# The low part of every other weight chunk: a subtraction on VectorE, or a negated copy on ScalarE with an adding DMA of GpSimd

## What is computed

```python
h = x
h = h + gla_mixer(rmsnorm(h, gla_norm), w_in, ...)     # h @ w_in [2048 x 6160], gated linear attention, @ w_out [2048 x 2048]
h = h + square(relu(rmsnorm(h, mlp_norm) @ w_up)) @ w_down   # [2048 x 8192], [8192 x 2048]
h = rmsnorm(h, final_norm)
proj = rmsnorm(h, norm_gain_2) @ w_in_2                # [2048 x 6144]
q, k, v, g_sb, x_lru, g_lru = split(proj)
y = concat(stick_breaking_attention(q, k, v) * silu(g_sb), rg_lru(conv(x_lru)) * silu(g_lru))
return h + y @ w_out_2                                 # [2048 x 2048]
```

## Time and profile before

| | us |
|---|---|
| two runs | 1515.21, 1518.2 |
| median of the runs | 1516.7 |
| profiled execution, first to last instruction (span) | 1514.3 |
| TensorE busy | 1497.6 |
| VectorE busy | 843.5 |
| ScalarE busy | 711.9 |
| GpSimd busy | 30.8 |

### The profile page before, as it was taken

The page is one execution under the profiler, slowest core; times in us unless marked ns, Lnnn a source line. Parts: engine busy times, 40 slices in busy tenths (PEclk is TensorE's granted clock), DMA queues, the critical chain, the costliest instruction groups (busy, mean ns, idle before and its releaser), DMA issues. The chain is left out here.

```text
span 1514.3 us, 19184 instructions
## 1 busy us (share of the span) xinstructions
PE 1497.6 (99%) x6826; PEld 1237.1 (82%) x6826; DVE 843.5 (56%) x872; ACT 711.9 (47%) x856; POOL 30.8 (2%) x54
## 2 busy tenths in 40 slices
PE   7999999999999999999999999999999999999998
PEld 6788888888888888888888888888888888888886
DVE  5555545555555545555555554555566776565653
ACT  5544544445444433443344433444654664565532
POOL 3000000000000000000000000000000011000000
PEclk9999999999999999999999999999999999999999
DMA  8455565657666666666666666666556566545564
GB/s 267 137 167 154 145 202 176 187 176 240 192 183 182 192 192 194 185 182 188 194 189 184 189 190 191 189 190 185 182 180 181 154 194 191 166 144 167 181 193 140
DMA packets 144721, 277.03 MB, mean 183 GB/s; under 512 B 10800, under 2 KB 10912, under 8 KB 144512
## 3 DMA queue, kind: packets, MB, share of 16 engines
q1 hardware_dynamic: 143056, 271.75, 59.3%
q0 software_dynamic: 1040, 3.07, 0.6%
q10 hardware_dynamic: 544, 1.05, 0.2%
HBM read 273.74 MB, written 2.10 MB: 182 GB/s over the span
## 5 line engine op out<-in xcount | busy, mean ns | idle before, releaser
L1003 DVE TENSOR_TENSOR w_lo<-raw,w_hi 128x1024 fp32r<-128x1024 f32 x508 | 620.2, 1225 | 610.7 <-ACT w_hi L706 609.3
L706 ACT ACTIVATE w_hi<-raw 128x1024 fp32r<-128x1024 f32 x508 | 537.0, 1059 | 731.7 <-PE acc L420 710.5
L418 PE MATMUL acc<-w_hi,xa_hi 128*128 128x512 f32 x1276 | 506.3, 397 | 1.6 <-issue 1.4
L420 PE MATMUL acc<-w_hi,xa_lo 128*128 128x512 f32 x1276 | 497.3, 390 | 0.0
L419 PE MATMUL acc<-w_lo,xa_hi 128*128 128x512 f32 x1276 | 496.7, 389 | 0.0
L418 PE MATMUL acc<-w_hi,xb_hi 128*128 128x512 f32 x768 | 300.1, 391 | 1.5 <-DVE w_lo L1003 1.5
L420 PE MATMUL acc<-w_hi,xb_lo 128*128 128x512 f32 x768 | 299.0, 389 | 0.0
L419 PE MATMUL acc<-w_lo,xb_hi 128*128 128x512 f32 x768 | 298.8, 389 | 0.0
L418 PEld LDWEIGHTS acc<-w_hi,xa_hi 128*128 128x128 f32 x1276 | 239.7, 188 | 52.0 <-issue 3.2
L420 PEld LDWEIGHTS acc<-w_hi,xa_lo 128*128 128x128 f32 x1276 | 239.5, 188 | 50.7
L419 PEld LDWEIGHTS acc<-w_lo,xa_hi 128*128 128x128 f32 x1276 | 239.9, 188 | 49.4 <-issue 1.9
(11 more groups left out here) (198 smaller groups left out, 513.1 us busy)
## 6 DMA issues: line engine op xcount, KB each, us to landing
raw<-in_mlp_w_up SPq DMA_DIRECT2D x128, 512.0 KB, 3.7
raw<-in_mlp_w_down SPq DMA_DIRECT2D x128, 512.0 KB, 4.4
raw<-in_gla_w_in SPq DMA_DIRECT2D x96, 512.0 KB, 3.8
raw<-in_w_in SPq DMA_DIRECT2D x96, 512.0 KB, 3.7
raw<-in_gla_w_out SPq DMA_DIRECT2D x32, 512.0 KB, 4.5
raw<-in_w_out SPq DMA_DIRECT2D x32, 512.0 KB, 4.7
result<-stage SPq DMA_DIRECT2D x8, 256.0 KB, 3.3
h<-in_x ACTq DMA_DIRECT2D x2, 512.0 KB, 6.4
```

Of the source, the lines that this page charges most:

```text
L418: pe.matmul(o, xh[:, kt, xs], w_hi[:, n % RING, k, :], start=kt == 0, stop=False)
L420: last = pe.matmul(o, xl[:, kt, xs], w_hi[:, n % RING, k, :], start=False, stop=kt == KT - 1)
L706: act.activation(w_hi[:, n % RING, :, :], raw[:, n % RING, :, :], ACT.Copy)\
L1003: dve.tensor_tensor(w_lo[:, n % RING, :, :], raw[:, n % RING, :, :], w_hi[:, n % RING, :, :].bitcast(F32), ALU.subtract).then_inc(lo_ready, 1)
```

## The change

Odd chunks from number 5 on get their low part in another way. ScalarE, right after the high part, writes a second, negated copy of the raw chunk into `w_lo`; in the fp32r type that is minus the high part (`minus_ready`). GpSimd then issues a DMA that adds the raw chunk onto `w_lo` in place (`accum_op=ALU.add`), rows of 4096 bytes, 128 of them; its landing raises `added[0]` or `added[1]`, one for each odd buffer. VectorE skips these chunks. TensorE waits for `hi_ready` and `added` at odd chunks and for `lo_ready`, which now counts fewer, at even ones. The load into an odd buffer waits for `added` of the chunk before it there. GpSimd's powers and its three loads move into one program with the adds, panel by panel. Even chunks and the first four are made as before.

```diff
+def lows(n):
+    return n // 2 + 1 + sum(i % 2 for i in range(min(n + 1, RING)))
+
+def sums_of(n):
+    return 16 * (n // RING)
...
             def load(c, n0, it, per, src):
                 n = n0 + c
-                if it is None:
-                    if n >= RING:
-                        sp.wait_ge(lo_ready, n - RING + 1)
-                elif n >= RING:
-                    sp.wait_ge(lo_ready, it * per + (n - RING + 1))
+                m = n - RING
+                if m >= RING and m % 2:
+                    had = sums_of(m)
+                    step = sums_of(m + per) - had
+                    sp.wait_ge(added[m % RING // 2], had if it is None else it * step + had)
+                elif m >= 0:
+                    had = lows(m)
+                    sp.wait_ge(lo_ready, had if it is None else it * (per // 2) + had)
                 sp.dma_start(raw[:, n % RING, :, :], src).then_inc(raw_in[n % RING], 16)
...
+            def sum_lo(t, c, it):
+                n = CH * t + RING + c
+                if n >= CH * PANELS or c % 2 == 0:
+                    return
+                pool.wait_ge(minus_ready, at(lambda q: CH // 2 * q + (c + 1) // 2, t, it))
+                pool.dma_start(w_lo[:, n % RING, :, :].bitcast(F32), raw[:, n % RING, :, :], accum_op=ALU.add,
+                               max_dma_last_dim=4096).then_inc(added[n % RING // 2], 16)
+
+            def run(t, it=None):
+                for c in range(CH):
+                    prev = KINDS[t - 1] if t else ""
+                    if (t, c) == (0, 7):
+                        power(ST_X)
+                    if prev == "v" and c == 4:
+                        power(ST_O + (t - 5) // 2)
...
+                    sum_lo(t, c, it)
+
+            for t in range(PANELS):
+                run(t)
...
-                pe.wait_ge(lo_ready, at(lambda q: CH * q + c + 1, t, it))
+                if n >= RING and c % 2:
+                    pe.wait_ge(hi_ready, at(lambda q: CH * q + c + 1, t, it))
+                    pe.wait_ge(added[n % RING // 2], at(lambda q: sums_of(CH * q + c), t, it))
+                else:
+                    pe.wait_ge(lo_ready, at(lambda q: lows(CH * q + c), t, it))
...
                 act.activation(w_hi[:, n % RING, :, :], raw[:, n % RING, :, :], ACT.Copy)\
                     .then_inc(hi_ready, 1)
+                if c % 2:
+                    act.activation(w_lo[:, n % RING, :, :], raw[:, n % RING, :, :], ACT.Copy, scale=-1.0)\
+                        .then_inc(minus_ready, 1)
...
             def split_lo(t, c, it):
                 n = CH * t + RING + c
-                if n >= CH * PANELS:
+                if n >= CH * PANELS or c % 2:
                     return
```

More of the change, by code:

```diff
@@ L190, in gated_block_kernel @@
         hi_ready, lo_ready = sem("hi_ready"), sem("lo_ready")
+        minus_ready = sem("minus_ready")
+        added = [sem(f"added{i}") for i in range(2)]
         chunk_used = sem("chunk_used")
@@ L375, in _ @@
             pool.wait_ge(consts, 3)
[L376 to L384, removed]
+            def sum_lo(t, c, it):
[12 more added lines that the diff above has]
+                        power(ST_O + (t - 5) // 2)
+                    if (t, c) == (FIRST_U, 2):
+                        power(ST_MLP)
+                    if (t, c) == (FIRST_X, 4):
+                        power(ST_FIN)
+                    if (t, c) == (FIRST_X, 6):
+                        power(ST_N2)
+                    if prev and prev in "KQ" and c == 2:
+                        power(ST_KQ + t - 1 - 50)
+                    if (t, c) == (FIRST_O + 1, 2):
+                        pool.wait_ge(chunk_used, CH * (FIRST_O + 1))
+                        pool.wait_ge(tp_lo, groups_before(FIRST_O + 1))
+                        pool.dma_start(fin_gain, final_norm.partition_broadcast(P)).then_inc(late_in, 16)
+                        pool.dma_start(lru_w[:, 0, :, :], lru_w_a_2[0].rearrange("g i j -> i g j")).then_inc(late_in, 16)
+                        pool.dma_start(lru_w[:, 1, :, :], lru_w_x_2[0].rearrange("g i j -> i g j")).then_inc(late_in, 16)
+                    sum_lo(t, c, it)
+            for t in range(PANELS):
+                run(t)
         @block.tensor
```

## The result

The changed kernel took 1804.8 and 1811.5 us, median 1808.2, against 1516.7 before: ratio 1.192, 95% interval 1.190 to 1.194. That is 292 us more, inside the forecast range (1565 to 1990) and 65 us above the forecast of 1743.

What follows compares the result with a forecast made beforehand. The prediction took TensorE to bound the kernel before, and the odd raw buffer's trip after: 4.6 + 2.0 + 0.5 + 6.4 = 13.5 us a round, times 118.5 plus 141 us outside, giving 1743 us, range 1565 to 1990.

Steps and rivals of the forecast that it cites:

- Nothing to gain on VectorE: VectorE loses 254 low parts, 311 us of busy time, none on the path: gain 0, at most TensorE's 5.1 us of waits.
- ScalarE is covered: ScalarE's 254 negated copies, 269 us, fit its idle time: cost 0, or a few microseconds at panel ends without that cover.
- GpSimd's issues are free: GpSimd's 254 DMA issues at 0.58 us each, 147 us, cost nothing.
- The odd raw buffer's trip sets the round: Load, two copies, handoffs and add in series take 13.5 us per four chunks, against 11.59; chance 0.63, own range 1600 to 1850.
- The signs it named: TensorE waits at odd chunks, 1.9 us a round; load queue waits for adds; VectorE near 532 us; add 5.5 to 7.5.
- the add: GpSimd's adding DMA, from issue to landed: 6.4 us of the round, the middle of 5.0 and 7.7.
- the load: Load of a raw chunk into an odd buffer: 4.6 us of the round, against a 3.9 us median in the MLP.
- the handoffs: Three handoffs, to the load queue, ScalarE and GpSimd, at 0.16 us each: 0.5 us of the round.
- The second count by the engines' time: Transfer engines' time for four loads and two adds, each add counted as two reads: 13.8 us a round, engines full.
- Hidden: Rival: load plus add at or under 9.1 us, TensorE stays full, 1514 to 1545 us; hidden or nearly, chance 0.15.
- Slow adder: Rival: the add's own rate decides; an 8.5 us add gives 15.6 us a round, 1990 us; chance 0.20 shared with clock.
- The clock: Rival named with the slow adder for times above 1850 us; shared chance 0.20.

Runs made afterwards that it cites:

- every fourth, copy first: Changed kernel with only every fourth chunk (buffer 1) using the adding DMA, negated copy written before the high part: 1535.6 us, ratio 1.012 to the kernel before.
- the kernel with the 7.0 us: Changed kernel with the DMA adding a constant in 4 KB rows instead of the raw chunk, load waiting only for ScalarE: 1725.2 us, ratio 1.137 to the kernel before.
- the last of these kernels: Changed kernel with the DMA adding a 4 KB-row constant, negated copy before the high part, load waiting for the high part: 1579.4 us, ratio 1.041 to the kernel before.

## Why the prediction was right, point by point

- *Nothing to gain on VectorE.* Right as far as is shown: 300 us of its work went, and no kernel here that relieves it is faster than the kernel before. No run relieves VectorE and does nothing else; that TensorE had only 16.7 us of idle is the argument.
- *ScalarE is covered.* Right in the MLP, and 9.5 us over all, of the size given, though half of it falls in the first 100 us. ScalarE is busy 938.5 us and not 981, as copies back to back overlap in the records (by 0.09 us in the trip above, 904.39 + 1.06 - 905.36).
- *GpSimd's issues are free.* Right as busy time, wrong as to price: 0.85 us each and not 0.58, and they lie on the trip, inside the add's latency.
- *The odd raw buffer's trip sets the round.* Right: its three handoffs hold only 1.1 of 13.64 us, TensorE waits at odd chunks, and a trip made shorter by a copy (minus 106 us), made shorter by a transfer that adds nothing (minus 164) or longer by shorter rows (plus 55) moved the run the way and about as far as 119 rounds say. With the add taken out of the trip, the next loop took over (1725 us), and with that one shortened as well the run came down to 1579.
- *The signs it named.* The load queue waits for adds; TensorE waits at odd chunks, 1.5 us a round and not 1.9; the transfer engines are 87% busy by the records; VectorE is busy 543 us where 532 were named. The add's 5.3 us (median) are just under the 5.5 to 7.5 named.
- *The sizes.* 13.5 us forecast, 13.98 measured, 57 of the 65 us that were missing (118.5 x 0.48). In the MLP the terms' errors cancelled: the add 1.0 us too long, the load 0.5 us too short, the handoffs 0.6 us too short, of which 0.44 is ScalarE getting to a landed chunk late and 0.17 GpSimd's start after a copy. The 0.16 us of one queue's handoff was taken for all three, and that was the term that was mis-sized by the largest factor. Outside the stretch from 600 to 1300 us the rounds are longer still: (1666 - 700) / (119.2 - 51.5) = 14.27 us. The forecast gave all rounds one length. By the starts of the high parts, chunks 32 to 127 had 11.94 us a round before and have 14.24 now, chunks 128 to 383 (the MLP) 11.20 and 13.65. Why the trip is longer outside the MLP isn't shown.
- *The second count by the engines' time, 13.8 us.* It came out close for the wrong reason. It took busy time of overlapping records for work that can't overlap; as many transfers of the same sizes went through in 11.5 us a round. Its doubling for an add was an estimate; against a copy the runs have 2.04 times the queue time.
- *The rivals.* Hidden: no, load and add are 10.6 us where 9.1 were needed. But the point at which it would be hidden was placed rightly: with a trip of 11.65 us (every fourth, copy first) 1.2% are left. Slow adder: no, the add takes twice the queue time of a copy, as two reads would, and not more. The clock, which shares a chance with the slow adder: it did fall in places, to a mean of 0.964 over the span, but the run stayed under 1850 us.

## What to carry to other kernels

Relieving an engine at half load gave nothing back here (VectorE, 56% busy, had 300 us less to do); ask instead what the new path's latency is added to. Add up the whole trip of a ring's buffer, from the release through every engine and queue back to the release, and compare it with the time in which the bound engine uses the ring up: well under it the trip should, by the author's estimate, cost nothing (the nearest case here, 11.65 us against 11.59, cost 1.2%), over it every microsecond cost about one for each turn of the ring (a trip 1.38 us shorter took 164 us off 119 turns). And when one loop is cut open, work out the next longest with the durations it will have then, not with those measured while the first one held things apart.

## What was not expected of the hardware

The add grows with the loads beside it: it took 5.3 us in the changed kernel, 7.0 us when the load was released by the same copy, and 6.1 us when the load came one copy later (medians). The loads didn't grow with it in the second case (4.9 and 5.3 us in the MLP, against 5.1 and 5.8 in the changed kernel) and did in part in the third (5.8 and 5.7). Sorted within the changed kernel by the loads in flight beside them, worked out from issue and landing times, adds with less than half a load beside them (in the mean over the add) took 4.57 us (44 adds), those with half to one 5.05 (71), those with one to one and a half 6.05 (79), those with more 6.48 (50). In the kernel with the 7.0 us most adds (185 of 244) have one and a half to two loads beside them, and took 7.14: most of the growth goes with the company, and what the rest is, stays open. It isn't simply the constant as the source, whose quickest add took 4.5 us in the last of these kernels, as that of the raw chunk did.

The mean of TensorE's granted clock over the span was 1.000 before and is 0.964 after. The trace's records of it hold two values, 1.00 and 0.50: 32 stretches of 3.4 to 10.2 us, 129.7 us in all, are at 0.50. There a 128x512 matmul starts every 0.43 us (from 932.24 to 935.23 us), and at 1.00 every 0.23 us (from 937.78 to 939.14 us). One such stretch, between its neighbours:

```profile
924.00:930.50 6.50, 2.98 (x12) 2.17 (x12) 1.98 (x2) 0.48 (x1) 0.00 (x0) 0.96 0.99 257
930.50:937.00 6.50, 6.20 (x15) 4.81 (x16) 1.23 (x1) 3.26 (x4) 0.84 (x1) 0.52 0.73 219
937.00:943.50 6.50, 6.50 (x35) 5.46 (x34) 1.56 (x2) 3.82 (x5) 0.85 (x1) 1.00 0.70 200
```

TensorE was busy 2.98 of 6.5 us and then had a granted clock of 0.52 in the mean: 15 matmuls in 6.5 us, where the next 6.5 us at 1.00 have 35. TensorE's busy time rose from 1497.6 to 1588.5 us with the same instructions. In the experiments the mean clock went roughly with the length of the run: 0.997 at 1527 and 1536 us, 0.983 at 1702, 0.986 at 1725, 0.954 at 1863. How much of the 292 us the slower matmuls caused themselves stays open: they can only act where ScalarE waits for TensorE (151.5 us in all, 132 times) or TensorE is behind its chunks, and no run held the clock up in the changed kernel.
